# Expert results added straight into the residual, the last group's 0/1 matrix formed early, and the next norm's token factor applied where the projections leave PSUM

## The reference, cut to what matters

```
x = x + gt2 * hier_moe(h)                  # 16 experts in 4 groups; a token uses 2 experts of 1 group
# second block
n    = rmsnorm(x, norms[0])                # x * rsqrt(mean(x*x) + eps) * g ; one factor r per token, one gain g per feature
proj = n @ w_in                            # split into q, kc, vc, ks, vs, kw, vw, gl, cb, cc, cx
kcmp, vcmp = compress(kc + pe), compress(vc + pe)    # 32-token windows, pe added, gelu(flat @ w1) @ w2
o_nsa  = nsa_attention(q, kcmp, vcmp, ks, vs, kw, vw, sigmoid(gl))
y      = sum_k conv_w[k] * shift(cc * cx, k)         # 3 taps along the tokens
o_conv = cb * y
```

## Time and profile before

| | us |
|---|---|
| three executions | 1886.65, 1890.35, 1897.05 |
| median | 1890.35 |
| the profiled execution, whole | 1897.58 |
| its span from first to last instruction | 1895.8 |
| granted TensorE clock, mean | 0.93 of full |

### The profile page before, as it was taken

How to read it: one execution, slowest core, us unless ns; L and a number is a source line. 1 busy time by engine, 2 the same in 40 slices (tenths; PEclk the granted TensorE clock), 3 DMA queues, 4 the chain that set the end, 5 groups by cost and what they waited for, 6 DMA issues and landing times. The chain is left out here.

```text
span 1895.8 us, 20726 instructions
## 1 busy us (share of the span) xinstructions
PE 1686.3 (89%) x7778; PEld 1320.3 (70%) x7778; DVE 888.7 (47%) x1407; ACT 495.2 (26%) x941; POOL 1003.5 (53%) x945
## 2 busy tenths in 40 slices
PE   4999798998979969999998699999887699999995
PEld 2778676766758747778876487666564388888884
DVE  7684754298682471231215862765366521111114
ACT  2201222303241120123443412433444410000011
POOL 2756653355716526758870345222373157677672
PEclk8999898898999979999998799999897799999997
DMA  9355311024213022424544532101221012322211
GB/s 357 151 194 191 103 62 64 23 82 165 76 45 113 22 109 91 150 84 155 187 154 182 212 100 89 45 24 45 67 82 53 22 67 89 111 89 92 109 67 45
DMA packets 32695, 197.55 MB, mean 104 GB/s; under 512 B 3735, under 2 KB 7591, under 8 KB 10964
## 3 DMA queue, kind: packets, MB, share of 16 engines
q1 hardware_dynamic: 26040, 179.57, 26.0%
q10 hardware_dynamic: 5836, 14.03, 2.3%
q0 software_dynamic: 720, 2.62, 0.4%
HBM read 190.90 MB, written 7.66 MB: 105 GB/s over the span
## 5 line engine op out<-in xcount | busy, mean ns | idle before, releaser
L2429 POOL TENSOR_TENSOR b_wlo<-b_raw,b_whi 128x512 fp32r<-128x512 f32 x516 | 703.9, 1371 | 69.2 <-ACT b_whi L1469 34.0
L2423 POOL TENSOR_SCALAR b_whi<-b_raw 128x512 fp32r<-128x512 f32 x420 | 304.9, 726 | 787.3 <-PE ps L436 602.2
L434 PE MATMUL ps<-b_hhi,b_whi 128*128 128x512 f32 (+1 forms) x1128 | 456.6, 405 | 28.6 <-DVE b_hlo L1684 15.5
L435 PE MATMUL ps<-b_hlo,b_whi 128*128 128x512 f32 (+1 forms) x1128 | 448.4, 398 | 0.0
L436 PE MATMUL ps<-b_hhi,b_wlo 128*128 128x512 f32 (+1 forms) x1128 | 447.1, 396 | 0.0
L434 PEld LDWEIGHTS ps<-b_hhi,b_whi 128*128 128x128 f32 x1128 | 218.6, 194 | 92.8 <-issue 45.2
L436 PEld LDWEIGHTS ps<-b_hhi,b_wlo 128*128 128x128 f32 x1128 | 218.5, 194 | 46.6
L435 PEld LDWEIGHTS ps<-b_hlo,b_whi 128*128 128x128 f32 x1128 | 218.7, 194 | 44.5 <-issue 0.7
L1217 ACT ACTIVATE b_arena<-ps 128x512 f32<-128x512 f32 (+6 forms) x126 | 68.2, 545 | 400.0 <-PE ps L436 323.7
L434 PE MATMUL ps<-b_ahi,b_whi 128*128 128x512 f32 x416 | 166.2, 400 | 4.5 <-DVE b_alo L1684 3.6
L435 PE MATMUL ps<-b_alo,b_whi 128*128 128x512 f32 x416 | 163.7, 394 | 0.0
(11 more groups left out here) (322 smaller groups left out, 2098.6 us busy)
## 6 DMA issues: line engine op xcount, KB each, us to landing
b_raw<-in_stream SPq DMA_DIRECT2D x165, 1024.0 KB, 4.8
bias_near<-bias_vectors ACTq DMA_DIRECT2D x1, 2298.0 KB
b_x<-in_xT SPq DMA_DIRECT2D x1, 2048.0 KB, 13.6
b_x<-in_xT ACTq DMA_DIRECT2D x1, 2048.0 KB, 7.7
h_tokens<-b_y ACTq DMA_DIRECT2D x1, 2048.0 KB, 11.7
b_arena<-in_cw ACTq DMA_DIRECT2D x1, 2048.0 KB, 7.2
out<-b_x SPq DMA_DIRECT2D x8, 256.0 KB, 2.0
bias_compressed<-bias_vectors ACTq DMA_DIRECT2D x1, 1024.0 KB
```

The source lines that it names most:

```text
L434: pe.matmul(o, ahi_, bhi_, start=start, stop=False)
L435: pe.matmul(o, ahi_, blo_, start=False, stop=False)
L2423: nc.gpsimd.tensor_scalar(whi[:, s, c], raw[:, r, c], 1.0, 1.0, ALU.mult, ALU.mult)\
L2429: nc.gpsimd.tensor_tensor(wlo[:, s, c], raw[:, r, c], whi[:, s, c].bitcast(F32), ALU.subtract)\
```

## The change

Three edits, with what follows from them.

1. The results of all four groups are multiplied by the gate and added straight into `X` as they leave PSUM (`added`); `Y` is not used for them.
2. The 0/1 matrix of rank 3 is formed before the last two weight pieces of that group, in columns of `ahi` that the one block does not use.
3. The token factor r is not applied to the input of the projections. ScalarE and VectorE split `X` times the gain as soon as a tile is complete. A new PE function, `linear_summed`, keeps four output banks open (kcvc, kskw) and goes by input tile: spread of tile k+1, then 12 projection matmuls for tile k, then the sum of squares of tile k. The weights of kcvc and kskw are laid out in that order. The factor is applied where outputs leave PSUM: on VectorE for kcvc, kskw, q2 and gl (`scaled`); on ScalarE, with the factor turned to one value per partition (four transposes, `rstdT`), for vsvw; and in the convolution once as r squared (cc times cx) and once as r.

```diff
+            def linear_summed(outs, tile_of, hi, lo, split_key, sum_key, ahead=None):
+                if ahead:
+                    ahead(0)
+                for key, frees in outs:
+                    o[key] = open_bank(key, frees)
+                total = open_bank(sum_key, "mean_square_read")
+                for k in range(KD):
+                    if ahead and k + 1 < KD:
+                        ahead(k + 1)
+                    pe.wait_ge(sem("lo"), SPLITS[split_key] + k + 1)
+                    for i, (key, _) in enumerate(outs):
...
+                        ins = three(o[key], whi[:, slot, c:c + P], wlo[:, slot, c:c + P],
+                                    hi[:, k, :], lo[:, k, :], k == 0, k == KD - 1)
...
+                    pe.wait_ge(sem("squares"), len(squares) + 1)
+                    ins = pe.matmul(total, ones, sq[len(squares) % 2], start=k == 0, stop=k == KD - 1)
...
-            spread_back(3)
-            share_banks(main=[0, 1, 2, 3, 4, 5], side=[])
-            norm_product("sum_n0", KD)
-            linear("kcvc", range(2), KD, hhi, hlo, 0, "kcvc_read", "n0")
-            linear("kskw", range(2), KD, hhi, hlo, 0, "kskw_read")
+            share_banks(main=[0, 1, 2, 3, 4, 5])
+            linear_summed([(("kcvc", 0), "kcvc_read"), (("kcvc", 1), "kcvc_read"),
+                           (("kskw", 0), "kskw_read"), (("kskw", 1), "kskw_read")], by_rows, hhi, hlo, "n0", "sum_n0",
+                          lambda d: spread_tile(3, d))
             linear_tokens("vsvw", 256, hhi, hlo, "vsvw_read")
+            pe.wait_ge(sem("rstd"), RSTDS_BY_N0)
+            o = open_bank("rstdT", "rstdT_read", "side")
+            for T in range(ST):
+                ins = pe.transpose(o[:, T * P:(T + 1) * P], rstd[:, T * P:(T + 1) * P], ident)
...
ScalarE:
             for k in range(KD):
-                act.wait_ge(sem("ffn1_added"), k + 1)
-                square_for("sum_n0", k, X[:, k, :])
+                hi_of("n0", k, hhi[:, k, :], src=X[:, k, :], ready=("spread_added", 2 * KD + k + 1),
+                      free=("spread", 3, min(k + 1, KD - 1)), gain=col("norms", k))
+                squares_of(1, lambda _: X[:, k, :])
             rstd_of("sum_n0", D)
...
-                for j in range(4):
-                    if i == conv_over(3 * j):
...
-                        evacuate(("conv", 3 * j), convc, "cc_read")
...
VectorE:
+            def added(key, d, name):
+                finished(dve, key)
+                run(V.scalar_tensor_tensor(X[:, d, :], bank(key), mod[:, 40 + d:41 + d], X[:, d, :],
+                                           op0=ALU.mult, op1=ALU.add), name)
...
                 if r == 3:
+                    tokens_of(3)
                     weight_lo(10)
...
             for k in range(KD):
-                spread_added(3, k)
-                run(V.scalar_tensor_tensor(X[:, k, :], Y[:, k, :], mod[:, 40 + k:41 + k], X[:, k, :],
-                                           op0=ALU.mult, op1=ALU.add), "ffn1_added")
-                add_squares_behind("sum_n0", k)
+                added(("spread", 3, k), k, "spread_added")
+                if k:
+                    n0_lo(k - 1)
+            n0_lo(KD - 1)
...
+            def scaled(key, dst, name, scale=1.0):
+                finished(dve, key)
+                run(V.scalar_tensor_tensor(dst, bank(key), scale, rstd, op0=ALU.mult, op1=ALU.mult), name)
 
             wait_rstd()
-            split("n0", KD, normed(KD, lambda k: X[:, k, :], norm_gain(0)), hhi, hlo)
+            for m in range(2):
+                scaled(("kcvc", m), kcvc[:, m, :], "kcvc_read")
+            for m in range(2):
+                scaled(("kskw", m), [ks2, kw2][m], "kskw_read")
+            run(V.tensor_tensor(rstd2, rstd, rstd, ALU.mult))
+            finished(dve, "rstdT")
+            run(V.tensor_copy(rstd_tok, tiles(bank("rstdT"), ST)[:, :, 0]), "rstdT_read")
+            for m in range(4):
+                scaled(("q2", m), q2[:, m, :], "q2_read", 0.125)
+            scaled(("gl", 0), glf, "gl_scaled")
             dve.wait_ge(sem("comp_in"), 16 * 3)
             for m in range(PIECE):
                 for i in range(2):
...
+                    if i == conv_over(3 * j):
+                        finished(dve, ("conv", 3 * j))
+                        finished(dve, "vcmp")
+                        run(V.tensor_tensor(convc, bank(("conv", 3 * j)), rstd2, ALU.mult), "cc_read")
...
                     if i == conv_over(3 * j + 2):
+                        run(V.tensor_tensor(y, y, rstd, ALU.mult), "rstd_used" if j == 3 else "step")
```

More of the change, by code:

```diff
@@ L883, in act_turned, with spread_tile, spread_back @@
                 mark(ins, ("act", r, e))
-            def spread_back(r):
+            def spread_tile(r, d):
                 blocks = range(RANK_BLOCKS[r])
                 pe.wait_ge(sem("token_of"), sum(RANK_BLOCKS[:r + 1]))
-                for d in range(KD):
[L890 to L896, removed]
+                pe.wait_ge(sem("out_lo"), outs_by(r, d // 4))
+                o = open_bank(("spread", r, d), "spread_added", "side")
+                for b in blocks:
+                    token_of = ahi[:, 0:4, token_cols(r, b)]
+                    pe.matmul(o, hhi[:, d, slot_cols(r, b)], token_of, start=b == 0, stop=False)
+                    ins = pe.matmul(o, hlo[:, d, slot_cols(r, b)], token_of, start=False, stop=b == blocks[-1])
+                mark(ins, ("spread", r, d))
+            def spread_back(r):
+                for d in range(KD):
+                    spread_tile(r, d)
             for r in (1, 2, 3):
@@ L1129, in finished @@
             eng.wait_ge(sem("matmuls_done"), done[key])
[L1131 removed]
+        PRODUCED = ("h1", "ya", "yb", "merged", "h2", "moe0", "conv", "nsa", "mem",
                     "n2", "n4")
@@ L1195, in rstd_of, with hi_of @@
                 run(nc.scalar.activation(dst, dst, ACT.Exp, scale=-0.5), "rstd")
-            def hi_of(key, i, dst, src=None, bias=None, ready=None, free=None):
+            def hi_of(key, i, dst, src=None, bias=None, ready=None, free=None, gain=1.0):
                 n = SPLITS[key] + i
@@ L1207, in hi_of @@
                 if bias is None:
-                    run(nc.scalar.activation(dst, src, ACT.Copy), "hi")
+                    run(nc.scalar.activation(dst, src, ACT.Copy, scale=gain), "hi")
                 else:
@@ L1556, in _ @@
                 act.dma_start(bct[32 * (h % 4):32 * (h % 4) + 32, h // 4, :], src).then_inc(sem("bias_cmp_in"), 16)
-            for m in range(2):
-                evacuate(("kskw", m), [ks2, kw2][m], "kskw_read")
+            act.wait_ge(sem("rstdT_read"), 1)
             for T in range(ST):
[L1560 to L1563, removed]
+                evacuate(("vsvw", T), vsw[:, T, :], "vsvw_read", w=256, scale=rstd_tok[:, T:T + 1])
+            table[0] = None
+            act.wait_ge(sem("gl_scaled"), 1)
+            run(nc.scalar.activation(glf, glf, ACT.Sigmoid), "gl_read")
             for i in range(2):
@@ L1675, in _, with lo_of @@
             V = nc.vector
-            def lo_of(key, i, dst, dst_hi, src=None, bias=None):
+            def lo_of(key, i, dst, dst_hi, src=None, bias=None, gain=None):
                 n = SPLITS[key] + i
@@ L1682, in lo_of @@
                 hi32 = dst_hi.bitcast(F32)
-                if bias is None:
+                if gain is not None:
+                    run(V.scalar_tensor_tensor(dst, src, gain, hi32, op0=ALU.mult, op1=ALU.subtract), "lo")
+                elif bias is None:
                     run(V.tensor_tensor(dst, src, hi32, ALU.subtract), "lo")
@@ L2178, in tokens_of, with n0_lo @@
             def tokens_of(r):
-                finished(dve, ("slot_out", r, 1, RANK_BLOCKS[r] - 1))
+                if r < 3:
+                    finished(dve, ("slot_out", r, 1, RANK_BLOCKS[r] - 1))
                 for b in range(RANK_BLOCKS[r]):
-                    run(V.tensor_scalar(ahi[:, 0:4, slot_cols(r, b)], tiles(count_up[:, 0:S], 4),
+                    run(V.tensor_scalar(ahi[:, 0:4, token_cols(r, b)], tiles(count_up[:, 0:S], 4),
                                         slot_w[:, RANK_SLOT[r] + b, 0:1], None, ALU.is_equal), "token_of")
-            def spread_added(r, d):
-                finished(dve, ("spread", r, d))
-                run(V.tensor_tensor(Y[:, d, :], bank(("spread", r, d)), Y[:, d, :], ALU.add), "spread_added")
+            def added(key, d, name):
+                finished(dve, key)
+                run(V.scalar_tensor_tensor(X[:, d, :], bank(key), mod[:, 40 + d:41 + d], X[:, d, :],
+                                           op0=ALU.mult, op1=ALU.add), name)
+            def n0_lo(k):
+                lo_of("n0", k, hlo[:, k, :], hhi[:, k, :], X[:, k, :], gain=col("norms", k))
             def weight_lo(j):
@@ L2202, in _ @@
                 for d in range(4 * h, 4 * h + 4):
-                    finished(dve, ("ed", d))
-                    run(V.tensor_copy(Y[:, d, :], bank(("ed", d))), "ed_read")
```

(5 more changed lines are left out.)

41 lines of the change are left out of this document (30 added, 11 removed).

## The result

| | before | after |
|---|---|---|
| median of four executions, us | 1890.94 | 1930.3 |
| lowest and highest, us | 1886.65, 1897.05 | 1921.85, 1934.39 |
| profiled execution: whole, span, us | 1897.58, 1895.8 | 1934.39, 1932.6 |
| granted clock, mean | 0.93 | 0.925 |

The ratio after/before is 1.0196, with a 95% interval of 1.0162 to 1.023: slower by 37 us on 1890.94. (The two medians differ by 39.4 us, the two profiled spans by 36.8.) The forecast was 28.1 us slower (1919 us), range 1903 to 1941.

What follows compares the result with a forecast made beforehand. TensorE, busy 89% of the span, bounds the kernel, with one hole of some 30 us before the projections. Terms 0.5 + 0 + 4.7 + 17.9 + 3 + 2 = 28.1 us on the median 1890.35 give 1919 us, range 1903 to 1941.

Steps and rivals of the forecast that it cites:

- Results into X, and the low part: Expert outputs added into X, +0.5 us (0 to 1.5); early matrix delaying the last expert's low part, 0 net.
- zero net: Early 0/1 matrix: PE stalls 0.7 us more at the last low part and wins 0.7 us back afterwards.
- The loop: Last expert matmul to token projection: steps of 6.2 us, then a 4.1 us bank wait; +4.7 us (-2 to +25).
- the start's 2.4: Loop start: PE, near idle before, runs the first 12 projection matmuls from half clock; 2.4 us.
- POOL's 1.5: Loop steps: POOL splits weights beside DVE, whose 0.69 us operations become 0.98; 1.5 us over the steps.
- Rival A: Loop falls to 1.2 GHz: 3.75 us more a step, 22 more in all, 1941 us; chance 0.13.
- Rival B: Behind gl, POOL does not disturb DVE: stall 13.2 us; loop starts without clock loss; 1908 us; chance 0.10.
- Rival C: DVE and ScalarE run ahead in the loop: step 4.1 us, not slower, 1890 us; chance 0.05.
- Rival D: Banks before the token projection bind PE to the norm again; 1 to 2 us extra; counted within the likeliest case's 0.72.
- The position sums: Behind gl: DVE's 32 sums lose their cover and PE stalls 17.9 us (13.2 to 25.5).
- The clock behind it: After the pause behind gl, PE restarts at half clock; +3 us (0 to 5).
- The attention: Attention beside the convolution: DVE gets eight multiplies by the factor or its square; +2 us (-2 to +6).

Runs made afterwards that it cites:

- e8: Changed kernel with the last group's 0/1 matrix formed at its old place, behind the output's split; 1932.6 us, 1.019 of the kernel before.
- e1: Changed kernel with the 32 position sums moved back under the projections on DVE; 1899.56 us, 1.0026 of the kernel before.
- e2: Changed kernel with the spread issued two tiles ahead instead of one in the loop; 1918.67 us, 1.0115 of the kernel before.
- e3: Changed kernel with both edits, position sums under the projections and spread two tiles ahead; 1882.77 us, 0.9917 of the kernel before.
- e4: Changed kernel with the first convolution tile's wide matmuls put ahead of the 64 narrow compression products; 1929.73 us, 1.0167 of the kernel before.
- e6: e3 without the four multiplies of y by the token factor in the attention; 1883.59 us, 0.9923 of the kernel before.
- e7: Kernel before with only DVE's 32 position sums made to wait for gl; 1927.17 us, 1.0159 of the kernel before.
- e9: e3 repeated in five rounds; 1883.69 us, 0.996 of the kernel before.
- e5: e3 with q2 ahead of the token projection vsvw and the sums in other portions; 1876.09 us, 0.9896 of the kernel before.
- e10: e5 repeated in five rounds; 1878.57 us, 0.994 of the kernel before.

## Why the prediction was right, and where it was wrong

The sign, the places and the largest term were right; one term was too small. By the marks, with the forecast in brackets, the terms measured: the loop with the matrix 6.2 us (4.7 + 0), the sums 19.2 (17.9), the clock behind them 9.5 (3), the attention 1.3 (2), the rest 0.6 (0.5). That is 36.8 against 28.1, and 6.5 of the 8.7 missing are the clock's.

**Results into X, and the low part (+0.5, 0).** The low part ended last again, as in the earlier trace rows, but PE waited 0.24 us for it and not 0.7 us more: DVE formed the matrix in slack before. So the step "zero net" had both of its sides wrong: the loss of 0.7 us did not come, and the early matrix is worth 2.4 us (e8), not 0.7. Most of that gain was already in the loop's term, whose start at 1067.0 us was drawn with the matrix early (1066.62 measured), so it is not taken off the sum once more.

```profile
1057.65 0.47 PE L441 MATMUL ps<-b_whi,b_ahi 128*128 128x512 f32 x1 [0.24 <-DVE b_alo L2201]
```

**The loop (+4.7).** Held: the stretch came out at +6.2, and e1, which has this part and not the sums, stands at +3.6 in the distance and some 5 us in time. The two differ by the clock: behind the bank wait the matmuls of the token projection were at half clock for 5.9 us in the changed kernel (1119.88 to 1125.76) and for 3.7 us in e1. First projection at 1066.62 (forecast 1067.0); a step at full clock 6.08 us (6.2), PE waiting 1.73 in it (1.9). The order in a step was as argued: spread, addition, low part, and nothing runs ahead, because spread k+1 stands behind the matmuls of k-1. DVE's and ACT's timeline of one step:

```profile
1086.79 0.72 ACT L1262 ACTIVATE b_hhi<-b_x,b_cols 128x512 fp32r<-128x512 f32 x1 [4.84 <-PE ps L940]
1086.80 0.75 DVE L2234 SCALAR_TENSOR_TENSOR b_x<-ps,b_mod,b_x 128x512 f32<-128x512 f32 x1 [4.51 <-PE ps L940]
1087.61 0.75 DVE L1727 SCALAR_TENSOR_TENSOR b_hlo<-b_x,b_cols,b_hhi 128x512 fp32r<-128x512 f32 x1
```

The price of the new addition, for which no row of before existed, is 0.75 us here (0.78 taken). The last sum ended at 1116.0, against 1111.6 plus the start's 2.4 and POOL's 1.5, which is 1115.5. (Six steps of 6.2 us are 37.2 and not 37.4, so the forecast's 1111.6 should read 1111.4.) The bank wait is 3.88 us (4.1), released by a scaling as said.

**Rival A (the loop at half clock).** It came true in part. The clock was at half for a part of three of the eight steps, 8.21, 7.51 and 7.65 us long, 5.1 us more than three of 6.08; 0.5 us of this is a longer wait for the low part (2.27 us for 1.73). Two of these steps are the start, 3.6 us over, for which I had 2.4 and a share of POOL's 1.5. The third began at half clock at 1094.77 and was back at full at 1098.5. The Trainium skill, "TensorE: Matmul & The Clock Gate", in its section on the second failure mode, expects such swings in a loop with brief waits at the banks; here the brief waits were for the low part, and the swings came, but cost 5 us and not 22.

**Rival B (the sums are cheap).** It failed at both of its conditions: the pause was 19.16 us and not 13.2, with additions that took longer beside POOL (below), and the clock was low at the start of the loop.

**Rival C (the loop closes the hole).** Its threshold was a step of 4.1 us. It could not happen in this order, as argued, but two tiles ahead it did: 4.08 us in e2 and e3. Its forecast of 1890 us was too low all the same: e2, which has the short step and the pause, took 1918.67 us, 1.15% above before. The rival's sum had the pause at its lower end and no price for the clock behind it. Only with the sums moved as well (e3) is the kernel faster than before.

**Rival D (bound to the norm by the banks).** The bank wait came, without the extra 1 to 2 us: two of DVE's scalings there took 1.42 us together, 0.71 each.

**The position sums (+17.9).** Held: 19.16 us. The price beside POOL was too low. Beside POOL, which ended 10.27 us after gl was taken (10.3 forecast), an addition took 0.92 us (7.35 / 8) and not 0.77; alone it took 0.37 from start to start (8.40 / 23), against 0.385. The DMA share is nearly the same in the two stretches below (0.38 and 0.35), so the difference goes with POOL's work. DVE by stretch in the changed kernel, L2313 only:

```profile
1164.60:1172.20 7.60, 7.35 (x8) 0.64 0.38 138
1172.40:1180.80 8.40, 7.62 (x23) 0.50 0.35 125
```

**The clock behind it (+3). This is the term that failed.** By the marks it cost 28.7 - 19.2 = 9.5 us, and its upper bound was 5. In the products alone it is 13.89 against 7.28 us in e4, 6.6 us; 2.4 lie in the convolution tile behind them, and 0.5 in the small position products ahead of them. The duration of a low clock was taken from the earlier trace rows, where wide matmuls ended it after 6 us. Here 64 narrow ones, 62 columns each, come first, and the clock stays at half through all of them. That I had their row and priced them at 0.115 us, their full-clock price, was the error. With 9.5 in place of 3 the sum is 34.6; with the loop's 6.2 and the sums' 19.2 as well it is 37.4. The ratio says 37, between 31 and 43.

**The attention (+2).** 1.3 us in the profiles (3.0 to its very last product), but e6 shows no cost of the multiplies of y. The stretch took 141 to 149 us over all kernels here, with or without them, with the clock dropping at different places of it. So this term was a guess that noise confirms as little as it refutes.

**What stays open.** The terms are read from one profile of each kernel, and a low clock comes and goes from one profile to the next, so single terms are good to a few microseconds only. The first term (results into X, +0.5) has no run of its own. Why the clock drops at certain places in the attention was not tried.

## What to carry to other kernels

When an edit makes an engine's in-order list wait for a later event, price everything behind that wait in the list, and look for operations there that do not need the event: here 32 sums behind gl cost 30 us, and moving them up turned a loss of 2% into one of 0.3%. Where a loop's producer passes through two other engines, try to run it two tiles ahead: here that shortened the step from 6.08 to 4.08 us and, with the sums moved, turned the loss into a gain. And when a pause drops the clock, price the work behind it at half clock by its kind, not by the time in which other work recovered.

## What the runs showed of the hardware

- The clock stayed at half for 13.9 us of back-to-back narrow matmuls (64 of 128x128 by 62 columns) in which PE counted as busy throughout, and came back only after 2.7 to 5.3 us of wide ones behind them (the changed kernel, e2, e7, e8); with wide ones directly behind the same pause it was back 6.1 us after the restart (e4). At full clock the same 64 products took 7.28 us, and the clock held through them (1.00 from 1187.4 to 1194.6 in e4).
- DVE's additions of 128x128 in SBUF took 0.92 us on average beside POOL's splits, and 0.37 without them, a factor of 2.5, where I had read two in the trace of before. Single ones took between 0.35 and 1.32 us.
- Executions shift by up to 12 us ahead of the changed place (last expert matmul at 1049.5 in e7, 1061.75 before, with the same code up to there). Distances between marks in a trace leave this shift out; e3 and its repetition e9 agree in them to 1.8 us, e5 and e10 to 0.3.
